# Reordering the recurrence's vector work at the middle of a two-sequence RG-LRU encoder layer

## The chip, the cores and the metric

The kernel runs on one core of one Trainium2 chip. The metric is the device time of one execution in microseconds (us). Engines are named as in the profile: PE (TensorE), DVE (VectorE), ACT (ScalarE), POOL (GpSimd) and SP (SyncE); ACTq and SPq are the queues on which ACT and SP issue DMAs.

## The reference, cut to what matters

One encoder layer is applied to two sequences, `x_sample` of 1024 positions and `x_prompt` of 512. It has a bidirectional gated linear recurrence (RG-LRU) of 1280 channels, a windowed attention, a mixture with layer norm, and a gated MLP. The part that the change touches is the recurrence:

```python
def rg_lru_scan(u, w_a, b_a, w_x, b_x, lam):
    r = sigmoid(block_diag_linear(u, w_a, b_a))          # 8 blocks of 160 channels
    i = sigmoid(block_diag_linear(u, w_x, b_x))
    log_a = LRU_C * r * log_sigmoid(lam)
    a = exp(log_a)
    bt = sqrt(-expm1(2.0 * log_a)) * (i * u)
    _, h = associative_scan(combine, (a, bt), axis=1)
    return h

u = depthwise_conv(u_lru, w_lru_conv, b_lru_conv, LRU_CONV_PAD)
h_fwd = rg_lru_scan(u, ...)                              # and h_bwd on the flipped sequence
y_lru = ((h_fwd + h_bwd) * gelu(g_lru)) @ w_lru_out
```

## The kernel before, in words

The layer runs first for the long sequence (`q` = 0, `T` = 1024) and then for the short one (`q` = 1, `T` = 512). Each has three phases, of which the first, "lru", holds the change. All engines run programs written out by hand and meet at counting semaphores; each engine's program is in order, so a wait holds everything behind it, the DMAs that this engine issues among it.

**Tiles of the recurrence.** The 1280 channels lie in 8 blocks of 160. The first 128 channels of each block are a tile of their own, and the remaining 32 of four blocks share a tile, the "remainder" (`REST_TILE`). So there are two halves (`h` = 0, 1) with four block tiles (`jj` = 0 to 3) and one remainder each. A tile has the number `n = 5 * h + jj`; the remainder of the first half is 4, the first block of the second half, written (1, 0) below, is 5. Block (1, 0) is `blk` 4 = `HALF`.

**Order on PE** (`order_lru`): after the first half come `gates(0,3)`, the channel projection `u(1,REST)`, `g(0,3)`, `u(1,1)`, `gates(1,0)`, `g(1,0)`, `u(1,2)`, `gates(1,1)`, `g(1,1)` and so on. A projection is 24 weight loads with three split products (line 877); a gate slab is five groups `m` = 0 to 4 (lines 927 and 930): two decay gates, two input gates, and the gates of the block's 32 remaining channels. The groups rotate through PSUM: for T = 1024 there are two places, so PE may begin group 2 of a slab only when ACT has read group 0; for T = 512 there are four places, so group 4 waits for group 0. PE begins a gate slab when `u_split` says that DVE has split the block's channels into head and tail.

**On ACT**, per block: four sigmoids (line 1396) from PSUM into `sig[0..3]` (0 and 1 are the decay gates r of the two directions, 2 and 3 the input gates i), a fifth into `sig_rest` (line 1402), which DMAs move into the four remainder tiles `sigr` (`move_rest_gates`, by SP for most blocks, by ACT for the last of a half); then `decays` (two tanh, two exp, two squares: lines 1360, 1363, 1368), `roots` (two square roots, line 1374), and `take` for the projections behind the gates (gelu on line 1332, convolution's first tap on line 1341). Before a block's four sigmoids, ACT waits on `scan_done` for both scans of the tile that used `sig` last (`side_user`): for T = 1024 that is the block just before, for T = 512 the one before that, since two blocks share a buffer side by side. The outputs are stored by `store_y` (line 583), a wait on `y_ready` and one DMA; that of the remainder (0, REST) is issued by ACT in block (1, 0), between `decays` and `roots`. The square of direction 1 goes to `sig_rest` for T = 1024, and for that waits on `rest_moved`, the end of the DMAs that read `sig_rest`; SP starts the DMAs of block (1, 0) only when the scans of (0, REST) are done, since they overwrite `sigr`.

**On DVE**, per tile: the channels' convolution (`convolve`, lines 1767 to 1771) and split (`split_channels`, lines 1780 and 1781), `decay_steps` (line 1784: two products i*u on lines 1786 and 1787, then two steps on the squares, line 1791), and `recur` (line 1794: for each direction a product, line 1799, and a scan, line 1801; then the sum, line 1802, and the product with the gelu, line 1807, which sets `y_ready`). At the middle the order before is: decay steps of (0, REST), convolution of (1, 1), scans and sum of (0, REST), split of (1, 1) (`split_next`), product of (0, REST), then all of (1, 0), then the convolution of (1, 2).

**POOL** splits the weights (lines 761 and 762) for the long sequence alone; the short one reads them from DRAM.

Of the kernel before, what the change touches and what calls it, by code (L numbers as in the profile page):

```python
# [24 lines left out]
ALU = mybir.AluOpType  # L25
ACT = mybir.ActivationFunctionType
# [5 lines left out]
BLOCKS = 8  # L32
# [101 lines left out]
def build(nc, A, out):  # L134
    ctx = ExitStack()
    with ctx:
# [437 lines left out]
                eng.dma_start(sigr[m][REST * jj:REST * (jj + 1), 0:T],  # L574
                              sig_rest[REST * m:REST * (m + 1), 0:T]).then_inc(rest_moved[q], 16)

        def square(d, T):

            if is_short(T):
                return sq[:, d * T:(d + 1) * T]  # L580
            return (sq, sig_rest)[d][:, 0:T]

        def store_y(eng, q, T, h, jj):

# [4 lines left out]
        with nc.Block() as block:  # L589
# [690 lines left out]
            def _(act):  # L1280
# [26 lines left out]
                for q, T in enumerate(SEQS):  # L1307
# [47 lines left out]
                    def decays(h, jj, r):  # L1355

                        n, tile = 5 * h + jj, feature_tile(h, jj)
                        for d in range(2):
                            act.wait_ge(y_stored[q], 16 * n)
                            A1(tau[n % 2][d][:, 0:T], r[d], ACT.Tanh, scale=decay_n[:, bass.ds(d * RT + tile, 1)]).then_inc(decay_done[q], 1)  # L1360
                        for d in range(2):
                            act.wait_ge(decay_done[q], 6 * n + d + 1)
                            A1(r[d], r[d], ACT.Exp, scale=decay_p[:, bass.ds(d * RT + tile, 1)]).then_inc(decay_done[q], 1)
                        for d in range(2):
                            act.wait_ge(decay_done[q], 6 * n + d + 3)
                            if d and jj < REST_TILE and not is_short(T):
                                act.wait_ge(rest_moved[q], 64 * (HALF * h + jj + 2))
                            A1(square(d, T), r[d], ACT.Square).then_inc(decay_done[q], 1)

                    def roots(h, jj):  # L1370
                        n = 5 * h + jj
# [16 lines left out]
                    for h in range(2):  # L1388
                        for jj in range(HALF):
                            blk = HALF * h + jj  # L1390
                            last = side_user(h, jj, T)
                            for m in range(4):
                                act.wait_ge(gate_full[q], 4 * blk + m + 1)
                                if last is not None:
                                    act.wait_ge(scan_done[q], 2 * last + 4)
                                A1(side(sig[m], jj, T), gate_psum(5 * blk + m, T), ACT.Sigmoid,  # L1396
                                   bias=col("b_gate", 8 * m + blk)).then_inc(gate_evac[q], 1)
                            act.wait_ge(slab_done, s0 + slab_at[("gates", h, jj)] + 3)
                            act.wait_ge(rest_moved[q], 64 * (blk + 1))
                            if h and jj == 0:  # L1400
                                roots(0, REST_TILE)
                            A1(sig_rest[:, 0:T], gate_psum(5 * blk + 4, T), ACT.Sigmoid,
                               bias=col("b_gate_rest", blk)).then_inc(gate_evac[q], 1)

                            if jj == HALF - 1:
                                move_rest_gates(act, q, T, h, jj)
                            if h and jj == 0:
                                store_y(act, q, T, 0, HALF - 1)
                            act.wait_ge(gate_evac[q], 5 * blk + 2 + gate_banks(T))
                            decays(h, jj, [side(r, jj, T) for r in sig[0:2]])  # L1410
                            if jj == HALF - 1:
                                store_y(act, q, T, h, jj - 1)
                            if h and jj == 0:
                                store_y(act, q, T, 0, REST_TILE)
                            if h == 0 and jj == HALF - 1:
                                take("u", 1, REST_TILE)
                            roots(h, jj)
                            if q == 0 and blk == 1:
                                repeat_rows()
                            if jj < HALF - 1:  # L1420
                                for e in behind_gates(h, jj):
                                    take(*e)
                        take("g", h, HALF - 1)
                        act.wait_ge(rest_moved[q], 64 * (HALF * h + HALF + 1))
                        decays(h, REST_TILE, [r[:, 0:T] for r in sigr[0:2]])
# [270 lines left out]
            def _(dve):  # L1696
# [52 lines left out]
                for q, T in enumerate(SEQS):  # L1749
# [31 lines left out]
                        tell(V.tensor_tensor(tail[:, 0:T], src[:, 0:T], head[:, 0:T].bitcast(F32), ALU.subtract),  # L1781
                             u_split[q], channel_at[(h, jj)] + 1)

                    def decay_steps(h, jj, r, i, chan):
                        n = 5 * h + jj
                        order(V.tensor_tensor(i[0], i[0], chan[:, 0:T], ALU.mult))
                        tell(V.tensor_tensor(i[1], i[1], chan[:, 0:T], ALU.mult), input_gated[q], n + 1)
                        for d in range(2):
                            dve.wait_ge(decay_done[q], 6 * n + 5 + d)
                            tau_d = tau[n % 2][d][:, 0:T]  # L1790
                            tell(V.scalar_tensor_tensor(out=tau_d, in0=square(d, T), scalar=1.0, in1=tau_d, op0=ALU.add, op1=ALU.mult),  # L1791
                                 q_ready[q], 2 * n + d + 1)

                    def recur(h, jj, r, i, gate, between=lambda: None):
                        n = 5 * h + jj
                        tau_j = [t[:, 0:T] for t in tau[n % 2]]
                        for d in range(2):
                            dve.wait_ge(root_done[q], 2 * n + d + 1)
                            order(V.tensor_tensor(i[d], i[d], tau_j[d], ALU.mult))
                            o, a, b = (z if d == 0 else z[:, ::-1] for z in (tau_j[d], r[d], i[d]))  # L1800
                            tell(V.tensor_tensor_scan(o, a, b, 0.0, ALU.mult, ALU.add), scan_done[q], 2 * n + d + 3)  # L1801
                        order(V.tensor_tensor(tau_j[0], tau_j[0], tau_j[1], ALU.add))
                        between()

                        dve.wait_ge(proj_evac[q], gelu_at[("g", h, jj)] + 1)
                        dve.wait_ge(y_stored[q], 16 * (n + 1))
# [14 lines left out]
                    for h in range(2):  # L1821
                        for jj in range(HALF):
                            blk = HALF * h + jj
                            if blk < BLOCKS - 1 and blk != HALF:

                                dve.wait_ge(slab_done, s0 + slab_at[("gates", h, jj)] + 3)
                                split_channels((blk + 1) // HALF, (blk + 1) % HALF)

                            dve.wait_ge(gate_evac[q], 5 * blk + 5 + gate_banks(T) - 1)
                            r_i = [side(z, jj, T) for z in sig]  # L1830
                            decay_steps(h, jj, r_i[0:2], r_i[2:4], u[jj % 2])
                            if blk == HALF - 1:
                                convolve(1, REST_TILE)
                                split_channels(1, REST_TILE)
                            recur(h, jj, r_i[0:2], r_i[2:4], side(gelu_g, jj, T))
                            if jj < HALF - 1 and blk + 2 < BLOCKS:
                                convolve((blk + 2) // HALF, (blk + 2) % HALF)
                        dve.wait_ge(rest_moved[q], 64 * (HALF * h + HALF + 1))
                        r_i = [z[:, 0:T] for z in sigr]
                        decay_steps(h, REST_TILE, r_i[0:2], r_i[2:4], ur[h])  # L1840
                        if h == 0:
                            convolve(1, 1)
                        recur(h, REST_TILE, r_i[0:2], r_i[2:4], gelu_gr[:, 0:T], split_next if h == 0 else (lambda: None))
                    end_phase(dve, end_of(q, "lru"))
                    if q:
                        dve.wait_ge(cleared, 1)
# [389 lines left out]
```

## Time and profile before

| what | value |
|---|---|
| median of 3 runs | 2744.3 us (2743.85 to 2744.9) |
| profiled execution, own time | 2745.17 us |
| profiled execution, span | 2743.4 us |
| PE busy | 2659.9 us, 97% of the span |
| DVE busy | 1486.2 us, 54% |
| ACT busy | 768.5 us, 28% |
| mean granted TensorE clock | 0.992 of full speed |

The lru phase of the long sequence runs to about 390 us of the span, that of the short one from about 1815 to 2000 us. In a timeline row the columns are start, duration, engine, line, operation, output and inputs, count, and in square brackets the idle time before and what ended it. A table by windows gives busy time (and count) of PE, weight loads, DVE, ACT and POOL, then the granted clock, the DMA share and GB/s.

### The profile page before, as it was taken

To read this page: it belongs to the slowest core of one execution; us is meant where nothing else is said; L and a number is where in the kernel's file an instruction comes from. 1 tells how busy PE (TensorE), PEld (TensorE's weight loads), DVE (VectorE), ACT (ScalarE), POOL (GpSimd) and SP (SyncE) were. 2 spreads that over 40 slices of the span, in tenths; PEclk is the share of its full clock that TensorE was granted. 3 is DMA by queue.
4 is the path that set the end of the run, shared out by engine and by line. 5 is a ranking of instruction groups with operands and counts; after the bars stand their busy time and mean duration, and the time that the engine had idled before them with its cause. 6 is when DMAs were issued, how large, how long until landed. Compare 5 with 4: busy or idle time off the path is not lost.

```text
span 2743.4 us, 32010 instructions
## 1 busy us (share of the span) xinstructions
PE 2659.9 (97%) x11898; PEld 2193.1 (80%) x11898; DVE 1486.2 (54%) x1780; ACT 768.5 (28%) x1053; POOL 653.2 (24%) x332
## 2 busy tenths in 40 slices
PE   8998999999999999999999999989999999999998
PEld 6786888888788877888888888878788778888886
DVE  6799754334504568644545464667742414644445
ACT  3565713313400022010101111148932301211112
POOL 3554532232133622434243332310000000000000
PEclk9999999999999999999999999999999999999999
DMA  6554554444596823435343433456656693544554
GB/s 216 198 196 157 200 184 157 173 161 168 201 375 230 314 87 129 157 133 180 129 181 124 177 129 147 148 210 219 227 199 229 218 355 134 207 184 187 198 199 166
DMA packets 168544, 519.94 MB, mean 190 GB/s; under 512 B 13255, under 2 KB 40135, under 8 KB 166384
## 3 DMA queue, kind: packets, MB, share of 16 engines
q1 hardware_dynamic: 113536, 422.02, 42.6%
q10 hardware_dynamic: 54896, 96.39, 9.9%
q8 instruction: 74, 1.21, 0.2%
q14 instruction: 38, 0.31, 0.0%
HBM read 303.13 MB, written 206.32 MB: 186 GB/s over the span
## 4 chain that ended last, share of the span: by engine, by line
PE 83%; DVE 10%; DMA 3%; ACT 3%; issue 1%; SPq 0%; ACTq 0%; DVEq 0%
PE ps L877 49%; PE ps L1218 12%; PE ps L1045 8%; PE ps L1139 4%; PE ps L927 3%; PE ps L1028 2%; PE ps L1078 1%; DMA gate_in<-gate_dram 1%; DMA W<-w_split 1%; PE ps L1065 1%; PE ps L930 1%; PE ps L1207 1%; DVE tau L1801 1%; DVE tau L1791 0%; DVE acc L2082 0%
## 5 line engine op out<-in xcount | busy, mean ns | idle before, releaser
L877 PE MATMUL ps<-XH,W 128*128 128x512 f32 x4224 | 1206.0, 391 | 26.9 <-DVE XL L1746 11.7
L877 PEld LDWEIGHTS ps<-XH,W 128*128 128x128 f32 x4224 | 794.8, 188 | 203.9 <-issue 19.6
L877 PE MATMUL ps<-XL,W 128*128 128x512 f32 x2112 | 710.0, 390 | 0.0
L877 PEld LDWEIGHTS ps<-XL,W 128*128 128x128 f32 x2112 | 397.9, 188 | 82.4
L1218 PE MATMUL ps<-W,HH 128*128 128x512 f32 x1152 | 310.1, 389 | 1.5 <-DVE HL L2065 1.5
L1218 PEld LDWEIGHTS ps<-W,HH 128*128 128x128 f32 x1152 | 216.1, 188 | 46.8 <-DVE HL L2065 1.9
L761 POOL TENSOR_SCALAR W<-raw 128x1024 fp32r<-128x1024 f32 (+2 forms) x72 | 91.4, 1270 | 566.8 <-PE ps L877 301.7
L1045 PE MATMUL ps<-XH,W 128*128 128x512 f32 x672 | 216.4, 393 | 0.0
L827 POOL TENSOR_SCALAR W<-raw 128x1024 fp32r<-128x1024 f32 x72 | 86.8, 1205 | 536.8 <-PE ps L877 228.8
L762 POOL TENSOR_TENSOR W<-raw,W 128x1024 fp32r<-128x1024 f32 (+2 forms) x72 | 205.6, 2855 | 6.0
L828 POOL TENSOR_TENSOR W<-raw,W 128x1024 fp32r<-128x1024 f32 x72 | 190.3, 2643 | 6.0
L1218 PE MATMUL ps<-W,HL 128*128 128x512 f32 x576 | 177.3, 389 | 0.0
L2077 DVE TENSOR_TENSOR acc<-ps,acc 128x1024 f32<-128x1024 f32 x60 | 73.5, 1225 | 163.0 <-PE ps L1218 158.9
L1045 PEld LDWEIGHTS ps<-XH,W 128*128 128x128 f32 x672 | 126.2, 188 | 25.5
L2052 DVE TENSOR_SCALAR v_conv<-v_raw,cols 128x1024 f32<-128x1024 f32 (+1 forms) x48 | 54.8, 1141 | 146.1 <-ACT v_raw L1658 144.7
L1658 ACT ACTIVATE g_raw<-ps,cols 128x1024 f32<-128x1024 f32 (+1 forms) x48 | 43.5, 906 | 314.2 <-PE ps L877 310.3
L1045 PE MATMUL ps<-XL,W 128*128 128x512 f32 x336 | 131.1, 390 | 0.0
L1218 PEld LDWEIGHTS ps<-W,HL 128*128 128x128 f32 x576 | 108.1, 188 | 22.5
L2052 DVE TENSOR_SCALAR g_conv<-g_raw,cols 128x1024 f32<-128x1024 f32 (+1 forms) x48 | 49.5, 1031 | 140.8 <-ACT g_raw L1658 138.6
L1658 ACT ACT_TABLE_LOAD x12 | 15.4, 1283 | 344.2 <-PE ps L877 335.5
L927 PE MATMUL ps<-u_head,W 128*128 128x512 f32 x240 | 85.7, 411 | 23.2 <-ACT sig L1396 16.3
L877 PE MATMUL ps<-ATH,W 128*128 128x512 f32 x384 | 108.2, 389 | 0.0
(205 smaller groups left out, 3341.8 us busy)
## 6 DMA issues: line engine op xcount, KB each, us to landing
w_split<-W SPq DMA_DIRECT2D x131, 1024.0 KB, 6.2
W<-w_split SPq DMA_DIRECT2D x130, 1024.0 KB, 6.8
raw<-w_mlp SPq DMA_DIRECT2D x72, 512.0 KB, 4.2
raw<-w_qkv_mix SPq DMA_DIRECT2D x28, 512.0 KB, 3.7
w_split<-W SPq DMA_DIRECT2D x8, 1280.0 KB, 12.3
W<-w_split SPq DMA_DIRECT2D x8, 1280.0 KB, 8.3
gate_dram<-mix_out ACTq DMA_DIRECT2D x16, 512.0 KB, 2.7
gate_in<-gate_dram ACTq DMA_DIRECT2D x16, 512.0 KB, 6.2
```

Of the source, the lines that this page charges most:

```text
L761: order(pool.tensor_scalar(half(0, slot, 0)[:, 0:width], raw[slot][:, 0:width], 1.0, 1.0, ALU.mult, ALU.mult))
L762: return pool.tensor_tensor(half(0, slot, 1)[:, 0:width], raw[slot][:, 0:width], half(0, slot, 0)[:, 0:width].bitcast(F32), ALU.subtract)
L827: order(pool.tensor_scalar(half(0, slot, 0)[:, 0:D_MODEL], raw[n % 2][:, 0:D_MODEL], 1.0, 1.0, ALU.mult, ALU.mult))
L828: pool.tensor_tensor(half(0, slot, 1)[:, 0:D_MODEL], raw[n % 2][:, 0:D_MODEL], half(0, slot, 0)[:, 0:D_MODEL].bitcast(F32), ALU.subtract). ...
L877: last = nc.tensor.matmul(bank(group, c), lhs(wl, k), rhs(xl, k, c), start=(k == 0 and n == 0), stop=(k == nk - 1 and n == 2))
L927: nc.tensor.matmul(ps[:, first + c, :], w[wl][:, m * P:(m + 1) * P], ut[xl][:, c * CH:(c + 1) * CH], start=(i == 0), stop=False)
L1045: last = nc.tensor.matmul(ps[:, 2 + side, :], half(q, slot_of(q, "attn", slab), wl)[:, k * P:(k + 1) * P], x_rhs(xl, k, c), start=(k == 0 ...
L1139: last = nc.tensor.matmul(ps[:, 2 * pair + f, :], X[q][xl][:, k, tt * P:(tt + 1) * P], half(q, slot_of(q, "w_o", k), wl)[:, f * CH:(f + 1) ...
L1218: last = nc.tensor.matmul(ps[:, 2 * pair + f, :], (HH, HL)[xl][:, kk, tt * P:(tt + 1) * P], half(q, DOWN_SLOT[kk], wl)[:, f * CH:(f + 1) * ...
L1658: A1(dst[:, 1:T + 1], psum(k, T), ACT.Identity, bias=col("b_up", FT * k + FG * g + n)).then_inc(up_evac[q], 1)
L2052: order(V.tensor_scalar(dst[:, 0:T], src[:, 0:T], col("fconv_w", tile), col("fconv_b", tile), ALU.mult, ALU.add))
L2077: tell(V.tensor_tensor(acc[:, tt, :], ps[:, bank:bank + 2, :].rearrange("p a b -> p (a b)"), acc[:, tt, :], ALU.add), down_added[q], nt * ...
```

## The change

`square` gets two more arguments: in the second half (`h` = 1) of the long sequence the square of direction 1 goes to `ur[0]`, the channels of the first half's remainder, and waits on `input_gated`, the products i*u of (0, REST), in place of `rest_moved`. The first sigmoid of each block (`m` = 0) waits for the first scan of the last user, the other three for both as before. ACT's `store_y` of (0, REST) moves from between the decays and the roots of (1, 0) to behind the roots and the `take` calls of (1, 0), ahead of the sigmoids of (1, 1). On DVE `decay_steps` is cut in `gate_inputs` and `decay_steps`, and `recur` in `scans` and `output`; at the middle the order becomes: decay steps of (0, REST), convolution of (1, 1), scans of (0, REST), products i*u and decay steps of (1, 0), split of (1, 1), scans of (1, 0), output (sum and product) of (0, REST), convolution of (1, 2), output of (1, 0). The numbers of instructions don't change.

```diff
--- before.py
+++ after.py
@@ -574,11 +574,11 @@
                 eng.dma_start(sigr[m][REST * jj:REST * (jj + 1), 0:T],
                               sig_rest[REST * m:REST * (m + 1), 0:T]).then_inc(rest_moved[q], 16)
 
-        def square(d, T):
+        def square(d, h, jj, T):
 
             if is_short(T):
                 return sq[:, d * T:(d + 1) * T]
-            return (sq, sig_rest)[d][:, 0:T]
+            return (sq, ur[0] if h else sig_rest)[d][:, 0:T]
 
         def store_y(eng, q, T, h, jj):
 
@@ -1364,8 +1364,11 @@
                         for d in range(2):
                             act.wait_ge(decay_done[q], 6 * n + d + 3)
                             if d and jj < REST_TILE and not is_short(T):
-                                act.wait_ge(rest_moved[q], 64 * (HALF * h + jj + 2))
-                            A1(square(d, T), r[d], ACT.Square).then_inc(decay_done[q], 1)
+                                if h:
+                                    act.wait_ge(input_gated[q], REST_TILE + 1)
+                                else:
+                                    act.wait_ge(rest_moved[q], 64 * (jj + 2))
+                            A1(square(d, h, jj, T), r[d], ACT.Square).then_inc(decay_done[q], 1)
 
                     def roots(h, jj):
                         n = 5 * h + jj
@@ -1392,7 +1395,7 @@
                             for m in range(4):
                                 act.wait_ge(gate_full[q], 4 * blk + m + 1)
                                 if last is not None:
-                                    act.wait_ge(scan_done[q], 2 * last + 4)
+                                    act.wait_ge(scan_done[q], 2 * last + (4 if m else 3))
                                 A1(side(sig[m], jj, T), gate_psum(5 * blk + m, T), ACT.Sigmoid,
                                    bias=col("b_gate", 8 * m + blk)).then_inc(gate_evac[q], 1)
                             act.wait_ge(slab_done, s0 + slab_at[("gates", h, jj)] + 3)
@@ -1410,8 +1413,6 @@
                             decays(h, jj, [side(r, jj, T) for r in sig[0:2]])
                             if jj == HALF - 1:
                                 store_y(act, q, T, h, jj - 1)
-                            if h and jj == 0:
-                                store_y(act, q, T, 0, REST_TILE)
                             if h == 0 and jj == HALF - 1:
                                 take("u", 1, REST_TILE)
                             roots(h, jj)
@@ -1420,6 +1421,8 @@
                             if jj < HALF - 1:
                                 for e in behind_gates(h, jj):
                                     take(*e)
+                            if h and jj == 0:
+                                store_y(act, q, T, 0, REST_TILE)
                         take("g", h, HALF - 1)
                         act.wait_ge(rest_moved[q], 64 * (HALF * h + HALF + 1))
                         decays(h, REST_TILE, [r[:, 0:T] for r in sigr[0:2]])
@@ -1781,17 +1784,19 @@
                         tell(V.tensor_tensor(tail[:, 0:T], src[:, 0:T], head[:, 0:T].bitcast(F32), ALU.subtract),
                              u_split[q], channel_at[(h, jj)] + 1)
 
-                    def decay_steps(h, jj, r, i, chan):
+                    def gate_inputs(h, jj, i, chan):
+                        order(V.tensor_tensor(i[0], i[0], chan[:, 0:T], ALU.mult))
+                        tell(V.tensor_tensor(i[1], i[1], chan[:, 0:T], ALU.mult), input_gated[q], 5 * h + jj + 1)
+
+                    def decay_steps(h, jj):
                         n = 5 * h + jj
-                        order(V.tensor_tensor(i[0], i[0], chan[:, 0:T], ALU.mult))
-                        tell(V.tensor_tensor(i[1], i[1], chan[:, 0:T], ALU.mult), input_gated[q], n + 1)
                         for d in range(2):
                             dve.wait_ge(decay_done[q], 6 * n + 5 + d)
                             tau_d = tau[n % 2][d][:, 0:T]
-                            tell(V.scalar_tensor_tensor(out=tau_d, in0=square(d, T), scalar=1.0, in1=tau_d, op0=ALU.add, op1=ALU.mult),
-                                 q_ready[q], 2 * n + d + 1)
-
-                    def recur(h, jj, r, i, gate, between=lambda: None):
+                            tell(V.scalar_tensor_tensor(out=tau_d, in0=square(d, h, jj, T), scalar=1.0, in1=tau_d,
+                                                        op0=ALU.add, op1=ALU.mult), q_ready[q], 2 * n + d + 1)
+
+                    def scans(h, jj, r, i):
                         n = 5 * h + jj
                         tau_j = [t[:, 0:T] for t in tau[n % 2]]
                         for d in range(2):
@@ -1799,8 +1804,11 @@
                             order(V.tensor_tensor(i[d], i[d], tau_j[d], ALU.mult))
                             o, a, b = (z if d == 0 else z[:, ::-1] for z in (tau_j[d], r[d], i[d]))
                             tell(V.tensor_tensor_scan(o, a, b, 0.0, ALU.mult, ALU.add), scan_done[q], 2 * n + d + 3)
+
+                    def output(h, jj, gate):
+                        n = 5 * h + jj
+                        tau_j = [t[:, 0:T] for t in tau[n % 2]]
                         order(V.tensor_tensor(tau_j[0], tau_j[0], tau_j[1], ALU.add))
-                        between()
 
                         dve.wait_ge(proj_evac[q], gelu_at[("g", h, jj)] + 1)
                         dve.wait_ge(y_stored[q], 16 * (n + 1))
@@ -1821,26 +1829,44 @@
                     for h in range(2):
                         for jj in range(HALF):
                             blk = HALF * h + jj
-                            if blk < BLOCKS - 1 and blk != HALF:
+                            r_i = [side(z, jj, T) for z in sig]
+                            if blk == HALF:
+
+                                output(0, REST_TILE, gelu_gr[:, 0:T])
+                                convolve(1, 2)
+                                output(1, 0, side(gelu_g, 0, T))
+                                continue
+                            if blk < BLOCKS - 1:
 
                                 dve.wait_ge(slab_done, s0 + slab_at[("gates", h, jj)] + 3)
                                 split_channels((blk + 1) // HALF, (blk + 1) % HALF)
 
                             dve.wait_ge(gate_evac[q], 5 * blk + 5 + gate_banks(T) - 1)
-                            r_i = [side(z, jj, T) for z in sig]
-                            decay_steps(h, jj, r_i[0:2], r_i[2:4], u[jj % 2])
+                            gate_inputs(h, jj, r_i[2:4], u[jj % 2])
+                            decay_steps(h, jj)
                             if blk == HALF - 1:
                                 convolve(1, REST_TILE)
                                 split_channels(1, REST_TILE)
-                            recur(h, jj, r_i[0:2], r_i[2:4], side(gelu_g, jj, T))
+                            scans(h, jj, r_i[0:2], r_i[2:4])
+                            output(h, jj, side(gelu_g, jj, T))
                             if jj < HALF - 1 and blk + 2 < BLOCKS:
                                 convolve((blk + 2) // HALF, (blk + 2) % HALF)
                         dve.wait_ge(rest_moved[q], 64 * (HALF * h + HALF + 1))
-                        r_i = [z[:, 0:T] for z in sigr]
-                        decay_steps(h, REST_TILE, r_i[0:2], r_i[2:4], ur[h])
+                        rests = [z[:, 0:T] for z in sigr]
+                        gate_inputs(h, REST_TILE, rests[2:4], ur[h])
+                        decay_steps(h, REST_TILE)
                         if h == 0:
+                            r_i = [side(z, 0, T) for z in sig]
+                            dve.wait_ge(gate_evac[q], 5 * HALF + 5 + gate_banks(T) - 1)
                             convolve(1, 1)
-                        recur(h, REST_TILE, r_i[0:2], r_i[2:4], gelu_gr[:, 0:T], split_next if h == 0 else (lambda: None))
+                            scans(0, REST_TILE, rests[0:2], rests[2:4])
+                            gate_inputs(1, 0, r_i[2:4], u[0])
+                            decay_steps(1, 0)
+                            split_next()
+                            scans(1, 0, r_i[0:2], r_i[2:4])
+                        else:
+                            scans(1, REST_TILE, rests[0:2], rests[2:4])
+                            output(1, REST_TILE, gelu_gr[:, 0:T])
                     end_phase(dve, end_of(q, "lru"))
                     if q:
                         dve.wait_ge(cleared, 1)
```

## Rows read from the trace of the kernel before

**Rows 1.** PE's waits over the whole span: in total, times, longest

```profile
PE ps L927 <- ACT sig L1396: 16.3, 3, 13.1
```

**Rows 2.** Timeline of PE, long sequence, around its longest gap

```profile
231.91 0.63 PE L930 MATMUL ps<-u_stack,gs 96*128 96x512 f32 x2
245.59 1.22 PE L927 MATMUL ps<-u_head,W 128*128 128x512 f32 x2 [13.05 <-ACT sig L1396]
...
248.32 1.05 PE L930 MATMUL ps<-u_stack,gs 96*128 96x512 f32 x2
```

**Rows 3.** Timeline of ACT, long sequence, same stretch

```profile
224.31 1.06 ACT L1368 ACTIVATE sig_rest<-sig 128x1024 f32<-128x1024 f32 x1 [5.39 <-DMA sigr<-sig_rest]
...
228.18 1.28 ACT L1374 ACT_TABLE_LOAD   x1 [2.81 <-DVE tau L1807]
...
243.13 1.28 ACT L1396 ACT_TABLE_LOAD   x1 [2.94 <-DVE tau L1801]
244.42 2.12 ACT L1396 ACTIVATE sig<-ps,cols 128x1024 f32<-128x1024 f32 x2
```

**Rows 4.** Timeline of DVE, long sequence, middle of the phase

```profile
220.08 1.56 DVE L1802 TENSOR_TENSOR tau<-tau,tau 128x1024 f32<-128x1024 f32 x1
...
225.31 2.47 DVE L1807 TENSOR_TENSOR tau<-tau,gelu_gr 128x1024 f32<-128x1024 f32 x1
227.81 1.22 DVE L1786 TENSOR_TENSOR sig<-sig,u 128x1024 f32<-128x1024 f32 x1
...
232.31 3.26 DVE L1791 SCALAR_TENSOR_TENSOR tau<-sig_rest,tau 128x1024 f32<-128x1024 f32 x1
...
240.45 2.29 DVE L1801 TENSOR_TENSOR_SCAN tau<-sig,sig 128x1024 f32<-128x1024 f32 x1
```

**Rows 5.** Timeline of POOL, long sequence, same stretch

```profile
229.80 1.41 POOL L761 TENSOR_SCALAR W<-raw 128x1024 fp32r<-128x1024 f32 x1 [3.10 <-DMA w_split<-W]
231.29 3.20 POOL L762 TENSOR_TENSOR W<-raw,W 128x1024 fp32r<-128x1024 f32 x1
```

**Rows 6.** Timeline of DVE, long sequence, a scan beside POOL

```profile
188.73 3.55 DVE L1801 TENSOR_TENSOR_SCAN tau<-sig,sig 128x1024 f32<-128x1024 f32 x1
```

**Rows 7.** Timeline of DVE, short sequence, middle of the phase

```profile
1926.00 0.69 DVE L1802 TENSOR_TENSOR tau<-tau,tau 128x512 f32<-128x512 f32 x1
...
1934.27 1.23 DVE L1801 TENSOR_TENSOR_SCAN tau<-sig,sig 128x512 f32<-128x512 f32 x1
...
1943.67 1.42 DVE L1791 SCALAR_TENSOR_TENSOR tau<-sq,tau 128x512 f32<-128x512 f32 x2 [1.33 <-ACT sq L1368]
```

**Rows 8.** Timeline of ACT, short sequence, same stretch

```profile
1928.76 0.61 ACT L1368 ACTIVATE sq<-sig 128x512 f32<-128x512 f32 x1
...
1934.87 1.28 ACT L1396 ACT_TABLE_LOAD   x1
1936.16 2.43 ACT L1396 ACTIVATE sig<-ps,cols 128x512 f32<-128x512 f32 x4
...
1939.03 1.35 ACT L1360 ACTIVATE tau<-sig,small 128x512 f32<-128x512 f32 x2
```

**Rows 9.** Timeline of PE, short sequence: its gaps

```profile
1936.90 0.50 PE L927 MATMUL ps<-u_head,W 128*128 128x512 f32 x1 [2.56 <-ACT sig L1396]
...
1982.06 0.50 PE L877 MATMUL ps<-XH,W 128*128 128x512 f32 x1 [1.96 <-ACT gelu_g L1332]
...
2172.87 1.09 PE L1065 MATMUL ps<-ident,probs 128*128 128x128 f32 x8 [3.43 <-DVE probs L1916]
```

**Rows 10.** Table by windows: granted clock is the third number from the end

```profile
1983.00:1987.00 4.00, 4.00 (x13) 3.08 (x12) 3.29 (x5) 3.97 (x7) 0.00 (x0) 0.57 0.43 176
...
245.59:249.17 3.58, 3.58 (x8) 2.81 (x9) 3.47 (x4) 0.95 (x1) 0.00 (x0) 0.50 0.00 0
1936.90:1941.00 4.10, 4.10 (x18) 3.39 (x19) 3.82 (x9) 4.08 (x7) 0.00 (x0) 1.00 0.37 125
```

**Rows 11.** All writes of the tau tiles: their stores' time to landing

```profile
DMA to landing us min/median/max: 2.0/2.9/6.5
```

## The prediction

> **What bounds the kernel now.** PE is busy for 97% of the span, so first I read which of its waits the change can reach. The list of PE's waits names one line of the recurrence: the gate slabs (line 927) wait 16.3 us for ACT's sigmoids, in three places, the longest 13.1 us [rows 1]. PE's timeline puts that one in the long sequence: two groups of `gates(1,1)` are done at 232.5, the third starts at 245.59 [rows 2]. The wait costs more than itself: the granted clock is 0.50, that is 1.2 GHz, for the 3.58 us behind it [rows 10], and a pair of matmuls takes 1.05 us, not 0.63 [rows 2]. ACT's timeline shows what the sigmoids wait for: the table load at 243.13 is released by the scan of (1, 0) that ends at 242.74 (240.45 + 2.29), and PE starts 245.59 - 242.74 = 2.85 us behind that [rows 3, 4]. DVE's timeline shows the chain: from 220.08 to 242.74 it runs twelve operations with no gap worth a name. In order they are the sum of (0, REST), cast and tail of the split of (1, 1), product of (0, REST), then for (1, 0) two products i*u, two decay steps, and product and scan twice [rows 4]. DVE is what ends last here. The short sequence has a smaller copy of the wait, 2.56 us [rows 9], but there ACT's own chain ends last: roots, gelu, first tap, and a table load at 1934.87, with the scans of (1, 0) over only at 1935.50 [rows 7, 8].
>
> **The change, part by part.** The sum is made against the profiled execution's own time, 2745.17 us; the median is 0.87 lower. Everything that isn't at the middle of the phase keeps its order.
>
> *The square in `ur[0]`.* ACT's square of direction 1 of (1, 0) waited 5.39 us for the DMAs of `sig_rest`, to 224.31 [rows 3]. It can now follow the other square, about 219 to 220, and this is what lets DVE take the decay steps early. On the path it is worth nothing by itself: DVE was busy throughout [rows 4].
>
> *DVE's order, long sequence.* Behind the scans of (0, REST), at 220.08, the same twelve operations run, in the order: two i*u, two decay steps, the split, product and scan twice, sum and product of (0, REST). The first scan of (1, 0) would then end four operations before the end. Not removed and not added: none, so the twelfth ends where it did, if POOL costs DVE as much. That is the one unknown. The decay step at 232.31 lasted 3.26 us; its neighbour POOL operation ended at 231.29 + 3.20 = 234.49, and the step 1.08 us later [rows 4, 5]. A scan beside POOL took 3.55 us, not 2.29 [rows 4, 6]. So both forms wait for POOL's operation to end and then run whole. POOL's programme hangs on PE's slabs and DMAs, which are unchanged up to here; so DVE loses the same, and y of (0, REST) is ready at about 242.7. I take 0. Bounds: 0.8 us earlier, if of the second pair of POOL operations DVE loses no more than the scan's 1.26 and one product's 0.7; 1.3 us later, if one more operation pays what that scan did.
> The Trainium skill, SBUF — State Buffer, in Who interferes with whom, says that a DVE instruction with two SBUF inputs contends with a POOL instruction that reads SBUF, and that the shared pair is held for the whole instruction. By that rule the term is 0; by a stretch in proportion (3.26 against 3.55 us) it would lie within the bounds above. The trace agrees with the rule.
>
> *ACT's order, long sequence.* Here the gain is lost. ACT issues the store of (0, REST) right ahead of the sigmoids of (1, 1), and the store waits for `y_ready`, which DVE now sets with the twelfth operation. The wait has a row: the same store held the square roots' table load to 228.18, 0.40 us behind the product that ended at 225.31 + 2.47 = 227.78, the DMA's issue within these 0.40 [rows 3, 4]. Behind the scan the load came 0.39 us late (243.13 - 242.74). So the new release is the old one in time, 242.7, and the load, the sigmoid and PE's start at 245.6 follow as before: 0. The relaxed wait of the first sigmoid for one scan is worth 0 too: where it would act, the store ends later, and in the other blocks PE's waits are the other two of rows 1, 3.2 us together, the larger in the short sequence.
> The roots, the gelu and the first tap of (1, 2) come earlier on ACT, hidden. The split of (1, 1) ends at about 230.3 by my order, some 5 us later than before, so PE may start `gates(1,1)` 1.6 us later; its two free groups take 3.7 us and need be done by 242.8: 0. Convolution of (1, 2), then output of (1, 0), end together where they did.
>
> *Short sequence.* From 1926.00 DVE runs its twelve without POOL, to 1935.50 [rows 7]. In the new order the decay steps come third, but ACT's squares end only at 1929.37 (1928.76 + 0.61) [rows 8]: two i*u end at 1927.4, DVE idles 1.5 us, and the twelfth ends at 1935.50 + 1.5 = 1937.0. The store holds ACT's sigmoids to that, and the table load starts at 1937.4, not 1934.87: +2.5 us. PE follows: its 2.56 us gap becomes about 1.1 (for the split) and 3.9 us. Queued behind ACT's wait are the sigmoids, hence `gates(1,1)`, hence all later slabs; nothing later in ACT, SP or DVE has another limit than these. The store must land before the output of (1, 0) and before the tanh of (1, 1): 2.9 us as a median, 6.5 at most [rows 11]. DVE has the convolution ahead of that, and later 1.33 us of idleness [rows 7] that grows to 1.33 + 2.5 - 1.5 = 2.3 us; the tanh, at 1939.03 before [rows 8], comes at 1941.5, 4.5 us behind the store: 0 at the median, 2 us at the maximum.
>
> *The clock behind the longer gap.* Rows bound it: gaps of 2.56 and 3.43 us stand in the trace [rows 9], and behind the first the clock stays 1.00 [rows 10]; behind one of 1.96 us [rows 9] it is 0.57 for 4 us, which costs 4 x 0.43 = 1.7 us [rows 10]. Behind 13.05 us it is low too. Between 0 and 1.8 (3.58 x 0.50) I take 1.7: the two gaps together are 5 us of idleness within 9.
> The Trainium skill, TensorE: Matmul & The Clock Gate, section HAM oscillation — how this bites in real kernels, holds that idle gaps of PE bring the clock down. By it the 1.7 us are spent; without it the sum would be +2.5.
>
> **Sum:** 0 + 2.5 + 1.7 = +4.2 us; 2745.17 + 4.2 - 0.87 = 2748.5 us.
>
> **The rivals.** *No clock loss* in the short sequence: +2.5, 2746.8 us. For it speaks the 2.56 us gap [rows 9, 10]; 0.30.
> *The reordering does what it says:* if the store did not hold the sigmoids, the first scan of (1, 0) would release them, four operations early: 1.22 + 2.29 + 1.22 + 1.22 and 0.1 of joints, 6.1 us, and nothing is lost in the short sequence: 2738.2 us. Against it stands the load at 228.18, held by this very store [rows 3]; 0.04.
> *Slower by more than the bound:* the low clock behind the short sequence's gaps lasts. Each us at it costs half; beside the 2.5 us it decides from 6 us of low clock on (3.0 us): 2745.17 + 5.5 - 0.87 = 2749.8 us or more, and 7 us make 2750.3. The stretch after the 13 us gap was 3.58 us [rows 10], after the 1.96 us gap about 4; for it speaks that PE now stops twice. POOL's upper bound of 1.3 would help it. 0.16.
> The forecast keeps 0.50.
>
> **How the numbers follow.** Two tenths of a per cent, 5.5 us, is about what a measurement of this kernel can tell from no change. Forecast and first rival lie within it: 0.80. Faster by more is only the second rival, 0.04; slower by more 0.16. The range goes from the first rival less 0.8 for POOL and 1.5 for the run's own spread and the clock in the long sequence, 2744.5, to the third at 7 us of low clock and half of POOL's bound, 2751.0.
>
> **What would show it.** In the profile after: ACT's table load ahead of the sigmoids of (1, 1) is released by the product of line 1807's successor, not by a scan, in both sequences, at about 243 and 1937. PE's long gap still ends near 245.6, and is cut by a short piece of work; the short sequence's gap is about 3.9 us. The square of (1, 0) direction 1 waits for nothing. Wrong would be: a table load released by the first scan at about 237 (the store doesn't hold it), or a long gap that ends over 1.5 us from 245.6 (POOL's part), or a clock of 1.00 behind the short sequence's gap.

## The result and the profile after

| | before | changed |
|---|---|---|
| median of 19 runs | 2744.81 us | 2750.02 us |
| lowest to highest | 2743.04 to 2748.33 | 2745.99 to 2753.02 |
| profiled execution, own time | 2745.17 | 2753.02 |
| its span | 2743.4 | 2751.2 |

The ratio is 1.0017, with a 95% interval of 1.0011 to 1.0023: the change costs 3 to 6 us, 5.2 by the medians. The profiled execution of the changed kernel is its slowest run, 3.0 us above the median, so the two spans differ by more (7.8 us) than the change is worth; the lines are read for the places where the two traces part, not for their sum. PE of the changed kernel ran 1.17 us ahead of the kernel before when it came to `gates(1,1)` of the long sequence, and 0.27 ahead at their last group; at `gates(1,1)` of the short sequence it was 1.83 us behind, and 7.01 at the end of that lru phase. So 0.9 us of the 7.8 arise at the middle of the long sequence and 5.2 in the short one from its middle on; the rest is spread over the remaining span and is not traced here.

**The long sequence.** DVE's timeline behind the second scan of (0, REST); the columns are those of the timeline rows before. The lines answer to [rows 4].

```profile
216.59 2.29 DVE L1806 TENSOR_TENSOR_SCAN tau<-sigr,sigr 128x1024 f32<-128x1024 f32 x1
218.91 1.56 DVE L1788 TENSOR_TENSOR sig<-sig,u 128x1024 f32<-128x1024 f32 x1
...
227.18 0.69 DVE L1783 CAST u_head<-u 128x1024 fp32r<-128x1024 f32 x1
...
231.15 4.36 DVE L1806 TENSOR_TENSOR_SCAN tau<-sig,sig 128x1024 f32<-128x1024 f32 x1
...
236.81 2.29 DVE L1806 TENSOR_TENSOR_SCAN tau<-sig,sig 128x1024 f32<-128x1024 f32 x1
...
240.39 1.23 DVE L1815 TENSOR_TENSOR tau<-tau,gelu_gr 128x1024 f32<-128x1024 f32 x1
```

The twelve operations start at 218.91 and end at 240.39 + 1.23 = 241.62, 22.7 us as before (220.08 to 242.74), only in another order: the first scan of (1, 0) now ends at 235.51, four operations ahead of the last. POOL's long operation beside it:

```profile
228.61 1.44 POOL L761 TENSOR_SCALAR W<-raw 128x1024 fp32r<-128x1024 f32 x1 [2.55 <-DMA w_split<-W]
230.13 3.23 POOL L762 TENSOR_TENSOR W<-raw,W 128x1024 fp32r<-128x1024 f32 x1
```

It ended at 233.36, and the scan 2.15 us behind it, 0.14 less than the 2.29 us it takes alone; the decay step in [rows 4, 5] ended 1.08 us behind its neighbour, also 0.14 less than its 1.22 alone. Both fit an operation that waits for POOL's to end and then runs whole. Now ACT's timeline of the changed kernel, which answers to [rows 3]:

```profile
217.77 1.04 ACT L1371 ACTIVATE ur<-sig 128x1024 f32<-128x1024 f32 x1
...
230.57 1.20 ACT L1341 ACTIVATE u<-ps,small,cols 128x1024 f32<-128x1024 f32 x1
241.65 0.33 ACTq L587 DMA_DIRECT2D y_dram<-tau  x1
242.37 1.28 ACT L1399 ACT_TABLE_LOAD   x1 [10.60 <-DVE tau L1815]
```

And PE's, which answers to [rows 2]:

```profile
229.24 0.70 PE L927 MATMUL ps<-u_head,W 128*128 128x512 f32 x2 [1.56 <-issue]
...
244.83 1.22 PE L927 MATMUL ps<-u_head,W 128*128 128x512 f32 x2 [11.66 <-ACT sig L1399]
```

The square into `ur` starts at 217.77, without a wait. ACT has no work from 231.77 (230.57 + 1.20) to 242.37: it stands at the store of (0, REST), which DVE releases at 241.62; the DMA is issued at 241.65, the table load follows 0.75 us behind the release, where it was 0.40 in [rows 3]. PE's one gap of 13.05 us is now two, 1.56 and 11.66 us, 13.2 together. Behind it the clock is a little lower than before, 0.73 against 0.79 over 9 us, or 0.5 us; with it the last group of `gates(1,1)` is 0.9 us later than before against the work ahead of the gap.

**The short sequence.** It starts with a wait that neither the description of the change nor the prediction names, though the diff has it: the wait for ACT's four sigmoids of (1, 0) (`gate_evac`) now stands ahead of DVE's convolution of (1, 1), where before it stood ahead of the products i*u of (1, 0). DVE's timelines at that convolution, of the kernel before and of the changed one:

```profile
1918.84 0.16 DVE L1767 TENSOR_TENSOR u<-u,small 128x2 f32<-128x2 f32 x1
```

```profile
1921.65 0.16 DVE L1770 TENSOR_TENSOR u<-u,small 128x2 f32<-128x2 f32 x1 [1.18 <-ACT sig L1399]
```

And ACT's, at the table load that follows the sigmoids of (1, 0), of the kernel before and of the changed one:

```profile
1920.00 1.28 ACT L1374 ACT_TABLE_LOAD   x1
```

```profile
1921.58 1.28 ACT L1377 ACT_TABLE_LOAD   x1
```

By ACT's load the changed kernel stands 1.58 us later at this point of the profile; DVE begins its twelve operations at 1928.36 in place of 1926.00, which is 2.36 us later. So the early wait costs DVE 0.78 us against ACT. DVE's timeline of the changed kernel from there, which answers to [rows 7]:

```profile
1928.36 0.69 DVE L1788 TENSOR_TENSOR sig<-sig,u 128x512 f32<-128x512 f32 x1
...
1930.53 1.42 DVE L1796 SCALAR_TENSOR_TENSOR tau<-sq,tau 128x512 f32<-128x512 f32 x2 [0.76 <-ACT sq L1371]
...
1937.86 0.69 DVE L1815 TENSOR_TENSOR tau<-tau,gelu_gr 128x512 f32<-128x512 f32 x1
...
1948.34 1.42 DVE L1796 SCALAR_TENSOR_TENSOR tau<-sq,tau 128x512 f32<-128x512 f32 x2 [2.52 <-ACT sq L1371]
```

ACT's timeline, which answers to [rows 8]:

```profile
1929.81 1.14 ACT L1371 ACTIVATE sq<-sig 128x512 f32<-128x512 f32 x2
...
1935.30 0.77 ACT L1341 ACTIVATE u<-ps,small,cols 128x512 f32<-128x512 f32 x1
1938.58 0.33 ACTq L587 DMA_DIRECT2D y_dram<-tau  x1
1939.00 1.28 ACT L1399 ACT_TABLE_LOAD   x1 [2.92 <-DVE tau L1815]
```

PE's timeline, which answers to [rows 9]:

```profile
1933.35 0.47 PE L927 MATMUL ps<-u_head,W 128*128 128x512 f32 x1 [1.05 <-issue]
...
1941.03 0.80 PE L927 MATMUL ps<-u_head,W 128*128 128x512 f32 x1 [3.72 <-ACT sig L1399]
...
1989.11 0.50 PE L877 MATMUL ps<-XH,W 128*128 128x512 f32 x1 [2.55 <-ACT gelu_g L1332]
```

ACT is through with the first tap of (1, 2) at 1936.07 and could load the sigmoid table then; it waits 2.92 us for the product on line 1815 (the output of (0, REST)), which ends at 1938.55. PE's gaps are 1.05 and 3.72 us, 4.77 in place of 2.56. A later gap of this phase, 1.96 us in [rows 9], is 2.55 us here.

The clock behind the gaps is read where PE works, since a low clock inside a gap costs nothing. The table by windows, with the granted clock as the third number from the end, of the 8.5 us behind each of the two gaps of the kernel before:

```profile
1936.90:1945.40 8.50, 8.50 (x37) 7.05 (x38) 6.51 (x12) 8.44 (x13) 0.00 (x0) 1.00 0.45 137
1982.06:1990.50 8.44, 8.44 (x30) 6.75 (x31) 6.42 (x10) 7.74 (x11) 0.00 (x0) 0.80 0.37 146
```

The same table of the changed kernel, with the 3.72 us gap itself as the first row:

```profile
1937.31:1941.03 3.72, 0.00 (x1) 0.00 (x0) 3.51 (x7) 2.02 (x3) 0.00 (x0) 0.76 0.81 322
1941.03:1949.50 8.47, 8.47 (x27) 6.83 (x28) 5.28 (x9) 8.00 (x12) 0.00 (x0) 0.70 0.34 89
1989.11:1997.60 8.49, 8.49 (x30) 6.84 (x31) 6.89 (x10) 8.20 (x12) 0.00 (x0) 0.80 0.33 132
```

The kernel before loses nothing behind its first gap and 8.44 x 0.20 = 1.7 us behind its second. The changed kernel loses 8.47 x 0.30 = 2.5 us behind the first and 8.49 x 0.20 = 1.7 us behind the second: 2.5 us more. The clock fell while PE still waited (0.76 over the gap).

### The profile page after: what moved, and what is told of

It reads as the page before. It is cut to its first block, busy times and chain, and to the rows that moved or that the text cites. A ratio compares the mean times of both kernels' runs of the same rounds, so it can differ in the third digit from the quotient of the medians.

```text
span 2751.2 us, 32008 instructions
## 1 busy us (share of the span) xinstructions
PE 2661.9 (97%) x11898; PEld 2195.0 (80%) x11898; DVE 1489.7 (54%) x1780; ACT 768.2 (28%) x1053; POOL 654.4 (24%) x332
## 4 chain that ended last, share of the span: by engine, by line
PE 82%; DVE 9%; DMA 4%; ACT 3%; issue 1%; SPq 0%; ACTq 0%; DVEq 0%
PE ps L877 49%; PE ps L1218 12%; PE ps L1045 8%; PE ps L1139 4%; PE ps L927 3%; PE ps L1028 2%; PE ps L1078 1%; DMA gate_in<-gate_dram 1%; DMA W<-w_split 1%; PE ps L1065 1%; PE ps L930 1%; DVE tau L1806 1%; PE ps L1207 1%; DVE acc L2108 0%; DVE acc L2110 0%
```

## The experiments

All were timed beside the kernel before on their chip; on those, its median was 2745.88 us for e1, e2, e3 and e5 and 2745.20 for e4, e6, e7 and e8, 33 runs each; each variant has 11. The diffs are against the changed kernel where nothing else is said.

### e1: the store behind the sigmoids of (1, 1)

```diff
                                     A1(side(sig[m], jj, T), ..., ACT.Sigmoid, ...).then_inc(gate_evac[q], 1)
+                            if h and jj == 1:
+                                store_y(act, q, T, 0, REST_TILE)
...
-                            if h and jj == 0:
-                                store_y(act, q, T, 0, REST_TILE)
```

> The changed kernel with ACT's store of (0, REST) moved from ahead of the four sigmoids of (1, 1) to behind them, in both sequences. My theory (the store's wait takes the place of the scan's): the table load ahead of the sigmoids is released by the first scan of (1, 0), PE's long gap ends near 239.5 us instead of 244.8, the short sequence's pair of gaps falls from 4.8 to about 2 us; about 6 us below the kernel before, 2738 to 2740, and about 11 below the change. Rival (DVE's total work sets the release whatever the store does): no more than 1 us below the change, about 2749.

Measured: 2739.45 us, ratio 0.9975 (0.9966 to 0.9984). ACT's timeline of e1, long sequence:

```profile
236.55 1.28 ACT L1399 ACT_TABLE_LOAD   x1 [3.84 <-DVE tau L1806]
237.84 1.11 ACT L1399 ACTIVATE sig<-ps,cols 128x1024 f32<-128x1024 f32 x1
240.15 1.11 ACT L1399 ACTIVATE sig<-ps,cols 128x1024 f32<-128x1024 f32 x1 [1.19 <-DVE tau L1806]
...
245.36 0.33 ACTq L587 DMA_DIRECT2D y_dram<-tau  x1
...
248.84 2.19 ACT L1360 ACTIVATE tau<-sig,small 128x1024 f32<-128x1024 f32 x2 [0.52 <-DMA y_dram<-tau]
```

PE's timeline of e1, its gaps in both sequences:

```profile
230.18 0.70 PE L927 MATMUL ps<-u_head,W 128*128 128x512 f32 x2 [1.60 <-issue]
...
239.01 1.22 PE L927 MATMUL ps<-u_head,W 128*128 128x512 f32 x2 [4.89 <-ACT sig L1399]
...
1926.61 0.47 PE L927 MATMUL ps<-u_head,W 128*128 128x512 f32 x1 [1.06 <-issue]
...
1931.39 0.50 PE L927 MATMUL ps<-u_head,W 128*128 128x512 f32 x1 [0.83 <-ACT sig L1399]
```

The table load is released by a scan (line 1806), PE's long gap is 4.89 us instead of 11.66, and in the short sequence the gaps are 1.06 and 0.83 (and a new one of 0.48 us a block later). One line moved on ACT is worth 10.6 us against the change (2750.02 - 2739.45; 11.5 by the ratios), with all of DVE's new order left in place. The rival, that DVE's total work sets the release, is out. The move has a small price of its own: the tanh of (1, 1) now waits 0.52 us for the store to land.

### e2: the short sequence as before

The branches that the change put in for the middle (DVE's order, the store's place) are taken only when `not is_short(T)`:

```diff
-                            if h and jj == 0:
+                            if h and jj == 0 and not is_short(T):
                                 store_y(act, q, T, 0, REST_TILE)
...
-                            if blk == HALF:
+                            if blk == HALF and not is_short(T):
```

> The changed kernel, but the short sequence keeps DVE's order and the store's place of the kernel before. My theory (the loss is in the short sequence, 2.5 us of waiting and 1.7 to 2.3 of low clock): within 1 us of the kernel before, 2744 to 2746; the short sequence's gap is 2.6 us again. Rival (the loss is in the long sequence, or is spread by other things such as DMA): stays at 2748 to 2750.

Measured: 2745.81 us, ratio 1.0004 (0.9995 to 1.0013): no difference from before, within an interval of -1.4 to +3.6 us. The short sequence's gap is 2.48 us again; the long sequence keeps the change's shape, 1.56 and 11.64 us. So in the long sequence the whole change is worth nothing that can be measured, and its loss, or most of it, is in the short one; e6 measures that from the other side.

### e3: the kernel before, and the first sigmoid waits for one scan

```diff
-                                    act.wait_ge(scan_done[q], 2 * last + 4)
+                                    act.wait_ge(scan_done[q], 2 * last + (4 if m else 3))
```

> The kernel before with one edit: the first sigmoid of a block waits for the first scan alone. My theory: in the order of before the relaxed wait does act, since the store is out of the way: the first scan of (1, 0) ends 3.6 us ahead of the second, ACT's own chain lets the table load start at about 240.2, and PE's gap ends about 2.9 us earlier; 2741 to 2742.5. Rival (as I wrote in the prediction, that the relaxed wait is worth 0): 2744.8.

Measured: 2742.44 us, ratio 0.9989 (0.9980 to 0.9998). ACT's timeline:

```profile
239.85 1.28 ACT L1396 ACT_TABLE_LOAD   x1
...
242.49 1.11 ACT L1396 ACTIVATE sig<-ps,cols 128x1024 f32<-128x1024 f32 x1 [0.22 <-DVE tau L1801]
```

And PE's:

```profile
242.31 1.22 PE L927 MATMUL ps<-u_head,W 128*128 128x512 f32 x2 [10.13 <-ACT sig L1396]
```

The load starts when ACT's first tap ends, at 239.84, not when a scan does, and PE's gap is 10.13 us and not 13.05: 2.9 us less, as expected. The forecast had the relaxed wait at 0, and inside the change the traces bear that out, since there the store (released at 241.62) ends later than the second scan (at 239.10); with the store out of the way it is worth something by itself.

### e5: e1 and e2 together

> Both edits together: the store behind the sigmoids of (1, 1) and the new order for the long sequence, all of the short sequence as before. My theory: 6 us below the kernel before, 2738 to 2739.5, and within 1 us of e1, as with the store out of the way the short sequence loses nothing by the order. Rival (the new order costs the short sequence something by itself, the later split of (1, 1)): e5 is 1 to 3 us below e1.

Measured: 2739.85 us, ratio 0.9978 (0.9969 to 0.9987), not to be told from e1. With the store behind the sigmoids the new order costs the short sequence nothing that can be measured; what cost it was the store's wait on that order.

### e4: the kernel before, and the square in `ur[0]`

> The kernel before with one edit: in the second half the long sequence's square of direction 1 goes to ur[0] and waits for the products i*u of (0, REST). My theory (DVE is busy throughout, the square's wait hid behind it): within 1 us of the kernel before; ACT's idle time ahead of that square falls from 5.4 us to none and PE's gap stays 13 us. Rival (the square was part of the chain): PE's gap gets shorter by 1 us or more and the time falls as much.

Measured: 2745.74 us, ratio 1.0000 (0.9991 to 1.0009). The square starts right behind the other, and PE's gap stays, as the timelines of ACT and PE in e4 show:

```profile
217.72 1.04 ACT L1371 ACTIVATE ur<-sig 128x1024 f32<-128x1024 f32 x1
...
244.47 1.22 PE L927 MATMUL ps<-u_head,W 128*128 128x512 f32 x2 [13.03 <-ACT sig L1399]
```

Its 5.4 us of waiting were hidden, and are no gain; the square is only what allows DVE's order.

### e6: the long sequence as before

The branches of e2, turned round; the first sigmoid's wait and the square stay as changed.

> The changed kernel, but here the long sequence keeps DVE's order and the store's place of before; the first sigmoid's relaxed wait and the square in ur[0] stay. My theory: the long sequence gains the 2.9 to 3.4 us of e3, the short one loses its 4 to 5 us: 1 to 2 us above the kernel before, about 4 us above e3; the short sequence's gaps are 1.1 and 3.7 us. Rival (the loss of the change was in the long sequence): equal to e3, about 3 us below the kernel before.

Measured: 2745.78 us, ratio 1.0002 (0.9993 to 1.0011), 3.3 us above e3 by the medians and 3.6 by the ratios ((1.0002 - 0.9989) x 2745). The intervals of the two ratios just touch (0.9993 to 0.9998), so by them alone the rival, equality with e3, is unlikely and not out; nine of e3's eleven runs lie below the lowest of e6. PE's timeline of e6 in the short sequence:

```profile
1928.00 0.47 PE L927 MATMUL ps<-u_head,W 128*128 128x512 f32 x1 [1.15 <-issue]
...
1935.69 0.80 PE L927 MATMUL ps<-u_head,W 128*128 128x512 f32 x1 [3.73 <-ACT sig L1399]
```

And its table by windows, behind this gap and behind the later one of 1.96 us:

```profile
1935.69:1944.20 8.51, 8.51 (x26) 6.85 (x27) 5.33 (x9) 8.03 (x12) 0.00 (x0) 0.68 0.34 90
1983.38:1991.90 8.52, 8.52 (x37) 7.06 (x38) 6.56 (x10) 7.87 (x11) 0.00 (x0) 1.00 0.47 144
```

The gaps are those of the changed kernel (1.15 and 3.73 us), 2.3 us more than e3's 2.56. The clock costs 8.51 x 0.32 = 2.7 us behind the long gap and nothing behind the later one, 1.0 us more than in the kernel before. Together that is 3.3 us, what the medians show.

### e7: e1, and the first sigmoid waits for both scans

> e1 (store behind the sigmoids) with the first sigmoid again waiting for both scans. My theory: in the long sequence the release moves from the first to the second scan of (1, 0), 3.55 us later; PE's gap is 8.4 us instead of 4.9, and the time 3 to 4 us above e1, about 2743. Rival (ACT's own chain, not the scan, sets the start as in e3): within 1 us of e1.

Measured: 2742.78 us, ratio 0.9991 (0.9982 to 1.0000), 3.3 us above e1 by the medians and 4.4 by the ratios. PE's gap is 8.45 us, 3.56 more than in e1, which is one product and one scan. The timelines of ACT and PE in e7:

```profile
239.58 1.28 ACT L1399 ACT_TABLE_LOAD   x1 [7.42 <-DVE tau L1806]
...
242.04 1.22 PE L927 MATMUL ps<-u_head,W 128*128 128x512 f32 x2 [8.45 <-ACT sig L1399]
```

So of the 6 to 7 us that e1 gains on the kernel before, a good half hangs on the relaxed wait, and the rest on the store's place and DVE's order together; no run parts these two.

### e8: e1, and the sigmoid table loaded ahead

Against e1:

```diff
+                            if h and jj == 0 and not is_short(T):
+                                A1(small[:, 155:156], conv_c[:, 0:1], ACT.Sigmoid)
```

The added sigmoid, of one column into an unused one, stands behind the `take` calls of (1, 0).

> e1 with one added sigmoid of a single column on ACT, long sequence only, behind the first tap of (1, 2), so that the sigmoid table is loaded while ACT waits for the first scan of (1, 0). My theory: the load of 1.28 us leaves the path, the first sigmoid starts 0.1 to 0.4 us behind the scan instead of 1.7, PE's gap falls from 4.9 to about 3.5 us; 1 to 1.7 us below e1, or more if the low clock stays away. Rival (PE's next groups then wait for the second scan's sigmoid, so the gap only moves on): within 0.5 us of e1.

Measured: 2739.02 us, ratio 0.9978 (0.9969 to 0.9987). The gap is shorter by 1.3 us, as meant; the timelines of ACT and PE in e8:

```profile
235.96 1.11 ACT L1399 ACTIVATE sig<-ps,cols 128x1024 f32<-128x1024 f32 x1 [2.32 <-DVE tau L1808]
239.55 1.11 ACT L1399 ACTIVATE sig<-ps,cols 128x1024 f32<-128x1024 f32 x1 [2.47 <-DVE tau L1808]
...
237.13 1.09 PE L927 MATMUL ps<-u_head,W 128*128 128x512 f32 x2 [3.59 <-ACT sig L1399]
```

but the timed runs don't show it: e8 lies 0.4 us below e1 by the medians and 0.8 above by the ratios, and its runs spread over 7 us (2735.45 to 2742.52). In the profile the second sigmoid still waits for the second scan, to 239.55, but the gain isn't lost by it: the last group of `gates(1,1)` starts 1.9 us earlier than in e1 when both are counted from the first group of `gates(1,1)`. Whether e8 is better than e1 stays open; both beat the kernel before by about 6 us, and the changed one by more.

## Why the prediction was right, point by point

The forecast was 2748.5 us in a range of 2744.5 to 2751.0, for a median of 2750.02. The chain that it named is the chain that is there. Of the 1.5 us by which it is low, 0.5 is the start: it built on 2744.3, the median of three runs, and the 19 runs give 2744.81. The change itself was put at +4.2 us and measured at +5.2.

- **DVE's order, long sequence (0).** The twelve operations took 22.71 us where they had taken 22.66. The bounds for POOL, 0.8 us earlier to 1.3 later, were not needed: the scan waited for POOL's operation to end and then ran whole, as the shared-pair rule of the Trainium skill (SBUF — State Buffer, Who interferes with whom) has it and as the rows had shown.
- **The store on ACT (0 in the long sequence).** The load is released by the product on line 1815 in both sequences, and e1 shows that this wait alone holds the gain. In the long sequence e2 puts the whole change at 1.0004, with 1 in its interval; the profile has 0.9 us there, of which 0.35 is the table load, 0.75 us behind its release and not 0.40. The second rival's price, 6.1 us below the kernel before if the store did not hold the sigmoids, is what e1 and e5 measured: 6.4 and 6.0 us. Its reason for failing was the one given.
- **The short sequence (+2.5).** The size was right, and the way to it only in part. The store's release was forecast 11.0 us behind the start of the twelve operations (1926.00 to 1937.0); it came 10.2 us behind it (1928.36 to 1938.55), since DVE idled 0.76 us before the decay steps and not 1.5. The other 0.78 us went into the wait ahead of the convolution of (1, 1), which the prediction overlooked. Both waits are on ACT's one chain, so their sum, 1.54 us, is what the prediction took for one of them. Against the table load behind the sigmoids of (1, 0), ACT's next sigmoid load comes at 17.42 us in place of 14.87: +2.55. The working has a slip here that did no harm: it names 1929.37, the end of both squares, which would give 2.0 us of idleness; 1.5 belongs to the end of the first square, 1928.85, which is all that the first decay step needs. PE's gaps are 1.05 and 3.72 us (forecast: 1.1 and 3.9), 2.2 us more than before.
- **The clock (+1.7).** The mechanism fits, and that the size is near is in part luck. The working added one low stretch of 1.7 us, the size of the one behind the 1.96 us gap. The changed kernel lost 2.5 us behind the 3.72 us gap and, like the kernel before, 1.7 behind the later one: +2.5. The profile of e6 lost 2.7 behind its 3.73 us gap and nothing behind the later one: +1.0. The forecast lies between the two. With 2.2 us of waiting this gives 4.7 us for the changed kernel, 5.3 with the 0.6 us by which the later gap grew, and 5.2 were measured. The Trainium skill's statement on idle gaps (TensorE: Matmul & The Clock Gate, HAM oscillation — how this bites in real kernels) agrees in kind.
- **The rivals.** The one without a clock loss is out for these profiles: behind the 3.7 us gap both the changed kernel and e6 ran at a low clock. The slower one, priced at 2749.8 us or more, has the measured median, 2750.02, within its price. Its condition was 6 us of low clock beyond that of before; the profile shows 5 (2.5 us lost at half speed), and the 0.5 us in the starting median did the rest. So the runs don't part it from the forecast as sharply as 0.16 against 0.50 suggests.

How much of the 5.2 us is waiting and how much is clock is known from profiled executions, one per kernel, and not from the timed runs; the split may differ between runs.

## What to carry to other kernels

When a wait is moved or relaxed, list everything that stands between the freed instruction and its engine's earlier work, DMA issues with their own waits included: here a store placed ahead of the sigmoids took the place of the wait that the reordering was to remove. Put an output's store on an in-order engine only behind the work that another engine waits for. And work a reordering out for every size that runs through the same code: what is neutral where DVE ends last is a loss where ACT does. Read the diff for waits that move with the work: one that was moved ahead of a convolution cost DVE 0.8 us here, and was in no list.

## What the runs showed that was not expected

The low clock does not belong to one gap. In the kernel before the short sequence had a gap of 2.56 us with a clock of 1.00 behind it and one of 1.96 us with a clock of 0.57 [rows 9, 10]. In e2, whose short sequence has the same order of work, it is the other way round, by its table by windows for the 8.5 us behind each gap:

```profile
1937.48:1946.00 8.52, 8.52 (x30) 6.91 (x31) 6.50 (x12) 8.46 (x13) 0.00 (x0) 0.80 0.46 131
1984.23:1992.70 8.47, 8.47 (x37) 7.02 (x38) 6.48 (x10) 7.79 (x11) 0.00 (x0) 1.00 0.44 142
```

The first stretch lies behind the gap of 2.48 us, the second behind that of 1.96 us. All eight profiles without the 3.7 us gap look like one of these two: a clock of 0.80 or 0.81 over 8.5 us, 1.6 to 1.7 us lost, behind exactly one of the two places. It is the first place in e2, e3 and e4, and the second in the kernel before, e1, e5, e7 and e8; in e1, e7 and e8 the gap at the first place is only 0.8 us. So behind gaps of about 2 to 2.5 us the same program may or may not lose the clock, and one profile doesn't say which gap is safe; but the loss at these two places together was the same. The two kernels with the 3.7 us gap lost more in both of their profiles, 4.2 and 2.7 us.
